# Mid-loop expert weights loaded as one 3 MB transfer per expert instead of gate/up and down apart

## What is computed

```python
scores = sigmoid(xt @ router_w)               # 256 tokens, 64 experts
e_idx, w = group_limited_top8(scores)         # 8 experts a token
for e in experts:                             # 64 experts of width 256
    hdn = silu(xs @ w_gate[e]) * (xs @ w_up[e])   # gate and up: 1024 x 256 each
    y   = hdn @ w_down[e]                         # down: 256 x 1024
    acc[tokens of e] += y * weight
out = acc + (silu(xt @ s_gate) * (xt @ s_up)) @ s_down   # one shared expert
```

## Time and profile before

| | us |
|---|---|
| runs of the kernel, median (lowest to highest of 3) | 1260.38 (1258.57 to 1262.38) |
| span of the profiled execution | 1256.4 |
| PE busy in it | 1193.9 (95%) |
| DVE, ACT busy | 407.5 (32%), 257.9 (21%) |
| DMA in the mean | 367 GB/s, 461.64 MB |

### The profile page before, as it was taken

The page is one execution under the profiler, slowest core; times in us unless marked ns, Lnnn a source line. Parts: engine busy times, 40 slices in busy tenths (PEclk is TensorE's granted clock), DMA queues, the critical chain, the costliest instruction groups (busy, mean ns, idle before and its releaser), DMA issues.

```text
span 1256.4 us, 15344 instructions
## 1 busy us (share of the span) xinstructions
PE 1193.9 (95%) x5946; PEld 604.9 (48%) x5946; DVE 407.5 (32%) x1096; ACT 257.9 (21%) x465; POOL 0.7 (0%) x9
## 2 busy tenths in 40 slices
PE   7999998859999999999999999997699999999998
PEld 6866444324444445444544654443244444444344
DVE  4756333112232222224311245322122222233242
ACT  1512221102211112112412411221111112112121
POOL 0000000000000000000000000000000000000000
PEclk9999999879999999999999999998899999999999
DMA  9955999999999999999822268999999999999990
GB/s 365 423 225 215 394 399 420 423 425 425 427 425 425 426 426 424 419 421 421 351 101 100 103 280 343 388 418 426 428 425 425 425 424 426 423 425 424 420 380 33
DMA packets 50042, 461.64 MB, mean 367 GB/s; under 512 B 5681, under 2 KB 6194, under 8 KB 8754
## 3 DMA queue, kind: packets, MB, share of 16 engines
q1 hardware_dynamic: 48816, 456.88, 87.4%
q10 hardware_dynamic: 1154, 3.79, 0.8%
HBM read 459.60 MB, written 1.05 MB: 367 GB/s over the span
## 4 chain that ended last, share of the span: by engine, by line
PE 78%; DMA 14%; SPq 3%; issue 3%; DVE 2%; ACT 0%; DVEq 0%
PE ps L491 75%; DMA weights<-in_experts 14%; SPq L343 2%; PE ps L578 1%; PE ps L748 1%; PE ps L755 1%; DMA weights<-in_win 1%; SPq L346 1%; DVE x_lo L1357 0%; DVE x_res L1286 0%; PE ps L894 0%; DVE sorting L1331 0%; SPq L387 0%; DVE z L1278 0%; DVE scratch L1278 0%
## 5 line engine op out<-in xcount | busy, mean ns | idle before, releaser
L491 PE MATMUL ps<-weights,xT 128*64 128x512 f32 (+3 forms) x2080 | 530.7, 601 | 43.9 <-issue 40.0
L491 PEld LDWEIGHTS ps<-weights,xT 128*64 128x64 f32 (+2 forms) x2080 | 183.4, 139 | 325.8 <-issue 314.7
L491 PE MATMUL ps<-weights,scratch 128*64 128x512 f32 (+2 forms) x1024 | 261.6, 597 | 1.2 <-DVE scratch L1446 1.2
L491 PE MATMUL ps<-scratch,xT 128*64 128x512 f32 (+2 forms) x384 | 157.6, 564 | 2.2 <-ACT xT L955 1.4
L491 PEld LDWEIGHTS ps<-weights,scratch 128*64 128x64 f32 (+2 forms) x1024 | 82.5, 136 | 112.1 <-issue 111.5
L1456 DVE SCALAR_TENSOR_TENSOR y_lo<-ps,slot_weight,y_hi 128x512 fp32r<-128x512 f32 x112 | 84.0, 751 | 152.6 <-ACT y_hi L955 152.6
L955 ACT ACTIVATE y_hi<-ps,slot_weight 128x512 fp32r<-128x512 f32 x112 | 76.7, 687 | 251.7 <-PE ps L491 238.9
L1443 DVE TENSOR_TENSOR scratch<-scratch,ps 128x256 f32<-128x256 f32 x56 | 23.6, 421 | 314.9 <-ACT scratch L955 314.9
L955 ACT ACTIVATE scratch<-ps 128x256 f32<-128x256 f32 (+2 forms) x68 | 26.7, 393 | 429.8 <-PE ps L491 423.1
L955 ACT ACTIVATE xT<-ps 128x512 f32<-128x512 f32 x132 | 77.5, 598 | 103.6 <-PE ps L491 84.9
L491 PE MATMUL ps<-onehot,x_hi 128*128 128x256 f32 x448 | 91.1, 289 | 0.9 <-DVE onehot L1365 0.9
(11 more groups left out here) (176 smaller groups left out, 687.9 us busy)
## 6 DMA issues: line engine op xcount, KB each, us to landing
weights<-in_experts SPq DMA_DIRECT2D x90, 2048.0 KB, 18.8
weights<-in_experts SPq DMA_DIRECT2D x140, 1024.0 KB, 24.0
scratch<-in_experts SPq DMA_DIRECT2D x18, 2048.0 KB, 20.2
scratch<-in_experts SPq DMA_DIRECT2D x24, 1024.0 KB, 21.8
weights<-in_pgate SPq DMA_DIRECT2D x8, 1024.0 KB, 27.6
weights<-in_wkv SPq DMA_DIRECT2D x8, 1024.0 KB, 26.4
weights<-in_win SPq DMA_DIRECT2D x7, 1024.0 KB, 20.5
weights<-in_shared SPq DMA_DIRECT2D x6, 1024.0 KB, 10.6
```

The lines of the kernel that those rows point to most:

```text
L491: return nc.tensor.matmul(out, lhsT, rhs, start=first, stop=last, skip_group_check=shared_bank)
```

## The change

For the places 8 to 55 (`whole(q)`: behind the resident ones, ahead of the tail, and not in a halved group) SP no longer issues gate/up and down apart. It waits, for each expert, until `down_mm` of the freeing group says that the slot's down matmuls are done, and then issues one transfer of the whole 3 MB (24 KB in each partition row). The transfer counts on `gu{j}_loaded`, with the same counts as before; PE no longer waits for `down{j}_loaded` in the groups of these places, and the counts for the other places come from a new table, `down_counts()`.

```diff
+def whole(q):
+    return RESIDENT < q < TAIL and IN_GROUP[q] not in HALVED
+
+def down_counts():
+    counts, table = [0] * 4, {}
+    for q in range(0, NE, 2):
+        if not whole(q):
+            counts[q // 2 % 4] += 32
+            table[q // 2] = counts[q // 2 % 4]
+    return table
...
                     else:
                         for p, w in zip(ps, weights):
-                            sp.wait_ge(S(f"gu_mm_{L}"), FREED_BY[p] + 1)
-                            gate_up(L, p, w)
+                            sp.wait_ge(S(f"down_mm_{L}"), 2 * FREED_BY[p] + 2)
+                            sp.dma_start(E(SLOT_OF[p]), w).then_inc(S(f"gu{p // 2 % 4}_loaded_{L}"), 16)
+                        continue
...
-                    for j, n in loads:
+                    for j, n in downs:
                         pe.wait_ge(S(f"down{j}_loaded_{L}"), n)
...
                     expert_group(g, g // 2, g % 2, [SLOT_OF[p] for p in ps] or [SHARED_SLOT],
-                                 [(p // 2 % 4, 32 * (p // 8) + 32) for p in ps[::2]], g == 0,
+                                 [(p // 2 % 4, 32 * (p // 8) + 32) for p in ps[::2]],
+                                 [(p // 2 % 4, DOWN[p // 2]) for p in ps[::2] if not whole(p)], g == 0,
```

More of the change, by code:

```diff
@@ L104 @@
 REST = rest_counts()
+DOWN = down_counts()
 assert sorted(SLOT_OF[TAIL:TAIL + 2]) == [0, 4] and sorted(SLOT_OF[TAIL + 2:]) == [5, 6]
@@ L687, in overflow, with expert_group @@
                        ).then_inc(S("over_mm"), 1)
-                def expert_group(g, it, b, slots, loads, first=False, own_gather=False, next_gather=False,
+                def expert_group(g, it, b, slots, loads, downs, first=False, own_gather=False, next_gather=False,
                                  shared=False, rests=(), rest_at=KC // 2, by_pairs=False):
@@ L791, in moe @@
                         expert_group(i * 2 + (GROUPS + b), i + ITERS, b, SLOT_OF[TAIL + 2 * b:TAIL + 2 * b + 2],
-                                     [((TAIL // 2 + b) % 4, i * 32 + (32 * ((TAIL // 2 + b) // 4) + 32))], own_gather=b == 0,
+                                     [((TAIL // 2 + b) % 4, i * 32 + (32 * ((TAIL // 2 + b) // 4) + 32))],
+                                     [((TAIL // 2 + b) % 4, i * 32 + DOWN[TAIL // 2 + b])], own_gather=b == 0,
                                      rests=[((TAIL // 2 + b) % 4, i * 32 + REST[TAIL // 2 + b])])
```

## The result

| | before | changed |
|---|---|---|
| runs, median (lowest to highest of 4 each) | 1259.74 us (1258.57 to 1262.38) | 1313.13 us (1310.49 to 1314.06) |
| ratio, 95% interval | | 1.0416 (1.0402 to 1.043) |
| span of the profiled execution | 1256.4 us | 1311.8 us |
| expert stage, layer 0 and layer 1 | 437.1, 435.8 us | 463.6, 463.5 us |

A stage counts here from the end of group 0's down matmuls to the end of the last group's. The stretch between the two stages took 202.2 us in both kernels and the tail 41.8 us. So the 55.4 us between the spans are 26.5 us in layer 0, 27.7 us in layer 1 and 1.2 us ahead of the first stage; where those 1.2 us come from stays open.

The account below looks back on a forecast made before the run. The DMA engines bound the kernel, so their idle time adds to it: net 25.1 us in layer 0 and 26.3 in layer 1, 51.4, less 2.4 for longer rows, gave 49 and a median of 1309 us; 8-in-10 range 1279 to 1328.

Parts of the forecast that it names:

- Gap 1: DMA engines idle while places 8 and 9 wait for group 1's down matmuls: 9.4 us layer 0, 10.6 layer 1.
- Gaps 2 and 3: DMA engines idle before places 12 and 13 flow, 0.3 us, and before places 14 to 17, 1.5 us.
- Gaps 4 and 5: DMA engines idle before places 20 to 23 and 26 to 29, behind groups 6 and 8: 4.8 us each.
- Gap 6: DMA engines idle before place 32, which waits for group 11: 2.2 us.
- Gap 7: DMA engines idle before place 36 flows, behind group 13's late end: 5.6 us.
- worse: Restart 5.4 us throughout, waits of 3 to 5 us at groups 4, 13, 19 also cost clock: 1330 us, chance 0.10.
- The clock: PE's lower granted clock after a wait of about 13 us adds 3.0 us to groups 6 and 8.
- The restart: Time from issue into an empty queue to full flow: 3.4 us, ends 2.7 and 5.4.
- Longer rows: 24 KB rows could give 428 GB/s, saving 0 to 4.8 us over 96 experts; 2.4 us taken.
- PE's waits: PE waits for landings ahead of groups 4, 6, 8 and 13: 3.3, 14.3, 16.4 and 5.4 us.
- only the start suffers: Rival: queue goes dry only at the first three gaps, depth covers the rest: 17 us together, 1277 us, chance 0.12.
- the faster side: Rival: no gap reaches the end, longer rows and fewer transfers bring 4.8 us: 1256 us, chance 0.03.

Follow-up runs that it names:

- second experiment: Kernel before, transfers issued as before, but PE waits for gate/up and down of the whole expert ahead of groups 4 to 24: 1260.4 us, ratio 1.0001.
- experiment with places 8 to 11: Kernel before with one 3 MB transfer an expert behind the down matmuls for places 8 to 11 (group 4) alone: 1272.54 us, ratio 1.0099.
- first experiment: Kernel before with gate/up and down still separate, both issued only behind the freeing group's down matmuls, PE's waits as before: 1276.49 us, ratio 1.0125.

## Why the prediction was right, step by step

- **What bounds the kernel.** Right. The second experiment moved PE's groups by 5.4 us without any change of the time, and the idle time of the DMA engines in the windows is found again in the stage (26.1 us worked out, or 27.0 with the window of before; 26.5 measured).
- **Gap 1** (predicted 9.4 and 10.6): 9.4 us in layer 0's window and 9.5 in layer 1's (216 GB/s from 811 to 830 us). It showed alone in the experiment with places 8 to 11, at 12.8 us for both layers after what the kernel before loses anyway (3.5 and 3.4).
- **Gaps 2 and 3** (0.3 and 1.5): 4.1 together. Too small; the start into an empty queue is paid again each time, however short the gap.
- **Gaps 4 and 5** (4.8 each): 4.5 and 3.6. The starts were 2.7 and 3.6 us against 3.4, and the clock cost less than counted.
- **Gap 6** (2.2): 3.3.
- **Gap 7** (5.6): 8.5, the term most mis-sized. Group 13 did wait about as long as said (4.96 against 5.4), but I gave the clock's price only to groups 6 and 8. Group 13's gate/up took 9.93 us in place of 7.1: 2.8 us were missing there, and gap 7 is 2.9 us too small. That waits of 3 to 5 us cost clock as well stood only in the rival "worse", with a chance of 0.10; this half of the rival came true.
- **Group 19**, "1.8 to spare": it waited 4.41 us, and a gap of 1.0 us followed that was not in the sum.
- **The clock.** Placed wrongly, nearly right in sum. Behind waits of 15.72 and 15.30 us gate/up took 248.49 - 239.76 = 8.7 and 295.94 - 286.87 = 9.1 us, 1.7 and 2.1 more than 7.0 and not 3.0; behind those of 4.96 and 4.41 us it took 9.93 and 9.31 us, 2.8 and 2.2 more than 7.1. The windows at half clock account for each (2.9, 2.2, 1.8, 2.1). At groups 6 and 8 the clock had been low since 226.2 and 274.0, 13 us ahead of the matmuls; at groups 13 and 19 it fell only at 366.2 and 461.8, 1.0 and 2.3 us ahead of them, and stayed low for longer into the matmuls, 5.8 and 4.4 us against 3.5 and 4.2.
- **The restart** (3.4, ends 2.7 and 5.4): 2.7, 3.6 and 3.0. The 5.4 did not come again, and it was misread: by the prediction's own rows the transfer was issued at 163.78 while the queue ran until 167.0, so it was no issue into a dry queue. Windows of the kernel before show the flow thinned there and not stopped, at 371 GB/s from 163 to 167 us and 366 from 167 to 170. The Trainium skill, page "DMA: Bandwidth & Descriptors", section "Anatomy of one DMA", gives about 2.0 us of fixed cost, for transfers issued on another path than SP's; the three starts measured here are all longer. Of the rule in the Trainium skill, same page, section "Rules for kernel authors" (issue early, wait late), the first experiment broke only the first half and cost 16 us; the second broke only the second half and cost nothing.
- **Longer rows** (0 to 4.8, taken 2.4): 431 against 425 GB/s, 4.8 us a layer by the rate, 9.6 in both. So the term was 7.2 us too small, and that hid most of the 34.4 - 28.6 = 5.8 us a layer by which the gaps were too small as well. The direct comparison, one transfer against two pieces, gave 4.5 us for both layers; by its rates, 427 and 431, it would be 6.6. The difference is not settled.
- **The time in sum.** 1309 us forecast, 1313 measured. That it is so close is partly luck: the gaps were 2 x 5.8 = 11.6 us too small and the rate's term 7.2 us too small, and the two errors have opposite signs.
- **PE's waits** (3.3, 14.3, 16.4, 5.4): 3.07, 15.72, 15.30, 4.96. Right within 1.5 us.

The net sum for layer 0 was 28.6 - 3.5 - 1.2 = 23.9 us against 26.5 measured, for layer 1 26.3 - 1.2 = 25.1 against 27.7. Of the rivals, "only the start suffers" was the first experiment's outcome; the faster side's gain is real, but it is a tenth of the cost.

## What to carry to other kernels

Where each slot is refilled by its reader's last use, look at the loop from landing to refill as a whole: waiting for all of a tile before the first use and refilling only after the last were worth 0 and 16 us alone, and 57 together. Bytes in the queue, not PE's idle time, say whether a delay costs anything: compare what the queue holds when the slowest group is read with that group's length plus one restart. Larger transfers bring their 1% only where the queue is deep enough to pay for the coarser hand-over, and each must be tried there: two of three such choices made new waits.

## What the runs showed of the hardware that I had not expected

- In a filled queue, rows of 24 KB flow at 431 GB/s, rows of 16 and 8 KB at 425 to 427, and rows of 8 KB at 420. The size of a transfer changes with them (3 MB, 2 and 1 MB, 1 MB), so no run here tells which of the two sets the rate.
- A wait of 4.4 to 5.0 us cost the matmuls behind it more (2.2 and 2.8 us) than waits of 15.3 and 15.7 us did (2.1 and 1.7), since they stood longer at a granted clock of 0.50 (4.4 and 5.8 us against 4.2 and 3.5).
- The first 3 MB transfer into a dry queue landed 2.7 to 3.6 us later than its bytes take at full flow. In the one looked at closely, bytes moved about 1 us after the issue, and the flow was full after 3 us.
- A float32 matmul of 128 columns by 512 stands in the trace as two records and takes 0.87 us (29.45 us for 34 of them).
